# Moving the accumulating transfers of the value projection from ahead of unit 4 to between units 8 and 17

## The reference, cut to what matters

```python
h = rmsnorm(x, pre_norm_g[l])                       # 512 tokens x 2048
proj = jnp.einsum('btd,dn->btn', h, w_in[l])        # 2048 x 7168
q, fz, iv, gate_a, u, ug, gate_b = jnp.split(proj, split_pts, axis=-1)
o_a = hgrn2_mixer(q, fz, iv, lower_bounds[l], hg_norm_g[l]) * jax.nn.silu(gate_a)
o_b = conformer_conv(u, ug, dw_k, dw_b, ln_g, ln_b) * jax.nn.silu(gate_b)
y = jnp.einsum('btm,md->btd', jnp.concatenate([o_a, o_b], -1), w_out[l])
x = x + rmsnorm(y, post_norm_g[l])
```

## Time and profile before

| | |
|---|---|
| time before, median of 3 runs | 862.48 us (861.43 to 863.76) |
| the profiled execution's own time | 862.48 us |
| its span | 860.8 us |
| PE busy | 847.0 us, 98% of the span |
| DVE, ACT, POOL busy | 643.1, 446.8, 402.5 us |
| chain that ended last | PE 95% |
| transfers | 119.15 MB; q1 (issued by SP) 88.24 MB, q0 (issued by POOL) 25.17 MB |

### The profile page before, as it was taken

How to read it: one execution, slowest core, us unless ns; L and a number is a source line. 1 busy time by engine, 2 the same in 40 slices (tenths; PEclk the granted TensorE clock), 3 DMA queues, 4 the chain that set the end, 5 groups by cost and what they waited for, 6 DMA issues and landing times.

```text
span 860.8 us, 12144 instructions
## 1 busy us (share of the span) xinstructions
PE 847.0 (98%) x4162; PEld 711.1 (83%) x4162; DVE 643.1 (75%) x1033; ACT 446.8 (52%) x692; POOL 402.5 (47%) x209
## 2 busy tenths in 40 slices
PE   8989999999999999999999999999999999999996
PEld 7978888888888888888888888888888888888885
DVE  5559779998989994957759486684947893787557
ACT  7843434444433357646647565474646843555442
POOL 3579688799747345342533425244242445032000
PEclk9999999999999999999999999999999999999998
DMA  9999875879404323141331314223131247888945
GB/s 308 256 226 223 216 171 132 199 179 203 144 26 127 93 75 115 57 122 50 98 97 49 97 53 119 72 73 97 53 117 49 74 162 200 225 144 174 270 193 195
DMA packets 127135, 119.15 MB, mean 138 GB/s; under 512 B 3408, under 2 KB 102009, under 8 KB 124537
## 3 DMA queue, kind: packets, MB, share of 16 engines
q1 hardware_dynamic: 117289, 88.24, 33.8%
q0 software_dynamic: 9056, 25.17, 16.0%
q10 hardware_dynamic: 752, 5.25, 1.6%
HBM read 103.96 MB, written 4.19 MB: 126 GB/s over the span
## 4 chain that ended last, share of the span: by engine, by line
PE 95%; POOL 2%; ACT 1%; issue 1%; DMA 1%; DVE 1%; SPq 0%; DVEq 0%; ACTq 0%; POOLq 0%
PE banks L1700 20%; PE banks L1702 19%; PE banks L1701 19%; PE banks L1733 6%; PE banks L1732 6%; PE banks L1734 6%; PE banks L1843 3%; PE banks L1844 3%; PE banks L1845 3%; PE banks L1764 1%; PE banks L1754 1%; PE banks L1612 1%; PE banks L1770 1%; PE banks L1798 1%; POOL w_lo L524 1%
## 5 line engine op out<-in xcount | busy, mean ns | idle before, releaser
L524 POOL TENSOR_TENSOR w_lo<-w_raw,w_hi 128x1024 fp32r<-128x1024 f32 x122 | 308.4, 2533 | 318.6 <-ACT w_hi L660 298.6
L1700 PE MATMUL banks<-h_hi,w_hi 128*128 128x512 f32 x736 | 292.3, 397 | 2.2 <-POOL w_lo L524 2.2
L1702 PE MATMUL banks<-h_hi,w_lo 128*128 128x512 f32 x736 | 287.8, 391 | 0.0
L1701 PE MATMUL banks<-h_lo,w_hi 128*128 128x512 f32 x736 | 287.4, 391 | 0.0
L1162 DVE SCALAR_TENSOR_TENSOR banks<-work,tap,banks 128x512 f32<-128x512 f32 x238 | 179.8, 755 | 7.9
L1700 PEld LDWEIGHTS banks<-h_hi,w_hi 128*128 128x128 f32 x736 | 138.8, 189 | 30.5 <-DVE work L1206 2.4
L660 ACT ACTIVATE w_hi<-w_raw 128x1024 fp32r<-128x1024 f32 x104 | 109.4, 1052 | 105.1 <-PE banks L1702 57.1
L1702 PEld LDWEIGHTS banks<-h_hi,w_lo 128*128 128x128 f32 x736 | 138.5, 188 | 29.3
L1701 PEld LDWEIGHTS banks<-h_lo,w_hi 128*128 128x128 f32 x736 | 138.8, 189 | 28.1 <-issue 0.5
L1843 PE MATMUL banks<-w_hi,h_hi 128*128 128x512 f32 x128 | 50.9, 397 | 0.0
L1845 PE MATMUL banks<-w_hi,h_lo 128*128 128x512 f32 x128 | 49.9, 390 | 0.0
(11 more groups left out here) (232 smaller groups left out, 1303.5 us busy)
## 6 DMA issues: line engine op xcount, KB each, us to landing
w_raw<-in_w_in SPq DMA_DIRECT2D x112, 512.0 KB, 3.8
w_raw<-in_w_out SPq DMA_DIRECT2D x32, 512.0 KB, 5.2
gates<-in_w_in POOLq DMA_DIRECT2D x12, 512.0 KB, 7.6
work<-in_w_out POOLq DMA_DIRECT2D x12, 512.0 KB, 10.1
work<-h_hi POOLq DMA_DIRECT2D x4, 1024.0 KB, 9.6
work<-h_lo POOLq DMA_DIRECT2D x4, 1024.0 KB, 10.6
mix<-in_x ACTq DMA_DIRECT2D x4, 1024.0 KB, 10.5
out_y<-mix SPq DMA_DIRECT2D x3, 1024.0 KB, 3.9
```

The source lines that it names most:

```text
L524: g.tensor_tensor(w_lo[:, a], w_raw[:, r * UW:(r + 1) * UW], w_hi[:, a].bitcast(fp32), ALU.subtract).then_inc(lo_done, 1)
L1700: mm(o, wh, hh, start=kt == 0, stop=False)
L1701: mm(o, wh, hl, start=False, stop=False)
L1702: ins = mm(o, wl, hh, start=False, stop=kt == KT - 1)
```

## The change

The four `v_bsum` loads are spread: one each after SP's load of units 8, 9, 10, 11. The two minus token adds go from ahead of unit 4 to behind the `w_lo` of units 8 and 9, the four P5 weight adds behind units 10, 11, 14, 16. The other four early token adds move as well: late_high_hi from 8 to 12, late_high_lo from 13 to 15, early_low_hi from 16 to 13, early_low_lo from 20 to 17. ACT makes the three negated copies behind its `w_hi` of units 6, 7 and 8, in the order first, minus, then, and both minus adds wait for all three. Nothing is added or removed in what is computed.

```diff
-    S_ADDS_AFTER = {8: ("then", "late_high_hi", 32), 13: ("then", "late_high_lo", 48),
-                    16: ("first", "early_low_hi", 32), 20: ("first", "early_low_lo", 48),
+    S_ADDS_AFTER = {8: ("first", "minus", 16), 9: ("then", "minus", 16), 12: ("then", "late_high_hi", 32),
+                    13: ("first", "early_low_hi", 32), 15: ("then", "late_high_lo", 48), 17: ("first", "early_low_lo", 48),
...
+        ADDS_AFTER[(10, 11, 14, 16)[u]] = ("P5", u)
...
-    BSUM_AFTER = 6
+    BSUM_AFTER = {8 + u: u for u in range(KT // 4)}
...
-                    pool.wait_ge(v_turned, 3 if to == "then" else 2)
+                    pool.wait_ge(v_turned, 3)
...
-            for u in range(HU):
-                v_add_weights("P5", u)
-            v_add_tokens("first", "minus", 16)
-            v_add_tokens("then", "minus", 16)
...
-            act.wait_ge(x_lo, 2 * KT)
-            A(v_minus, late_low_lo, ACT.Copy, scale=-1.0).then_inc(v_turned, 1)
-            A(v_first, late_low_hi, ACT.Copy, scale=-1.0).then_inc(v_turned, 1)
-            act.wait_ge(par_t, 1)
-            A(v_then, late_low_hi, ACT.Copy, scale=-1.0).then_inc(v_turned, 1)
...
+                if s == 4:
+                    act.wait_ge(x_lo, 2 * KT)
+                    act.wait_ge(par_t, 1)
+                    A(v_first, late_low_hi, ACT.Copy, scale=-1.0).then_inc(v_turned, 1)
+                if s == 5:
+                    A(v_minus, late_low_lo, ACT.Copy, scale=-1.0).then_inc(v_turned, 1)
+                if s == 6:
+                    A(v_then, late_low_hi, ACT.Copy, scale=-1.0).then_inc(v_turned, 1)
```

More of the change, by code:

```diff
@@ L431, in conv_load @@
                         in_unit(n, r % RING, half, (COL_UG if name == "UG" else COL_U) + j * P)
-                if n == BSUM_AFTER:
+                if n in BSUM_AFTER:
+                    u = BSUM_AFTER[n]
                     sp.wait_ge(x_ss, 3)
-                    for u in range(HU):
-                        sp.dma_start(v_bsum[u].rearrange("p (k c) -> p k c", c=512),
-                                     w_in[0, v_rows(u), ds(COL_V2, 512)].rearrange("(k p) c -> p k c", p=P)).then_inc(v_in[u], 16)
+                    sp.dma_start(v_bsum[u].rearrange("p (k c) -> p k c", c=512),
+                                 w_in[0, v_rows(u), ds(COL_V2, 512)].rearrange("(k p) c -> p k c", p=P)).then_inc(v_in[u], 16)
             def x_load(tt):
@@ L732, in _ @@
                 x_hi_part(1, k)
-            late_low_hi, late_low_lo = (quarter(h, 1, 0).bitcast(fp32) for h in (h_hi, h_lo))
-            act.wait_ge(x_lo, 2 * KT)
-            A(v_minus, late_low_lo, ACT.Copy, scale=-1.0).then_inc(v_turned, 1)
-            A(v_first, late_low_hi, ACT.Copy, scale=-1.0).then_inc(v_turned, 1)
-            act.wait_ge(par_t, 1)
-            A(v_then, late_low_hi, ACT.Copy, scale=-1.0).then_inc(v_turned, 1)
             act.wait_ge(lb_v, 1)
@@ L769, in v_turn @@
             def v_turn(s):
+                late_low_hi, late_low_lo = (quarter(h, 1, 0).bitcast(fp32) for h in (h_hi, h_lo))
+                if s == 4:
[6 more added lines that the diff above has]
+                    A(v_then, late_low_hi, ACT.Copy, scale=-1.0).then_inc(v_turned, 1)
                 if s == 27:
```

## The result

The changed kernel takes 869.32 us (median of 5 runs, 867.4 to 872.36), the kernel before 862.48 us in the same sitting (5 runs, 861.43 to 863.76). The ratio is 1.0077, with a 95% interval from 1.0050 to 1.0103: slower by 0.8%. Forecast were 867.0 us, own range 864 to 869, wide range 858.0 to 868.5. The sign and the place of the loss are as forecast; the time lies above both ranges.

A forecast was written before the change was run, and what follows sets the result against it. PE was taken as the bound, in flight for 98% of the span. 862.5 - 2.3 (unit 4 wait) - 1.7 (clock) + 6.8 (unit 14 wait) + 1.7 (clock) = 867.0 us; range 864 to 869, wide 858.0 to 868.5.

The forecast's parts named there:

- The wait at unit 4: PE's wait for weights ahead of unit 4 goes, as ACT's copies no longer stand ahead: 2.3 us gained.
- The clock there: PE's slow clock behind its wait at unit 4 should not occur: 1.7 us gained.
- A: First minus token add, behind unit 8 in POOL's queue: issued at 57.3, landing at 65.7 us.
- B: Second minus token add, behind unit 9 in POOL's queue: issued at 62.1, landing at 70.9 us.
- w0: First P5 weight add, behind unit 10 in POOL's queue: issued at 66, landing at 73.5 us.
- w1: Second P5 weight add, behind unit 11 in POOL's queue: issued at 69.5, landing at 76.1 us.
- C: Token add late_high_hi, behind unit 12 in POOL's queue: issued at 73, landing at 81.4 us.
- D: Token add early_low_hi, behind unit 13 in POOL's queue: issued at about 78, landing at 86.6 us.
- Rival 1: Loads hold their share beside POOL's adds, PE never waits after unit 3: 858.5 us, chance 0.32.
- The wait: PE waits at unit 14 for its load, held by POOL's adds and landing at 88.0: 6.8 us lost.
- Rival 2: Short waits of 1 to 4 us at unit 14 or units 15 to 18: 862.5 us, chance 0.17.
- rival 3: The wait at unit 4 stays and the queue does no harm: 862 us, chance 0.05.

The follow-up runs named there:

- e2: Changed kernel with the four v_bsum loads and four P5 weight adds back where the kernel before has them: 859.12 us, ratio 0.9958.
- e5: Changed kernel with e2's edits, and early_low_hi and early_low_lo behind units 18 and 22 in place of 13 and 17: 858.7 us.
- e9: Kernel before with 10 idle matmuls on PE ahead of unit 4: 862.08 us, ratio 0.9994.
- e3: Changed kernel with each token add issued as two transfers with 2 KB rows in place of one with 8 KB rows: 874.59 us.
- e6: Changed kernel with early_low_hi issued behind unit 14 in place of unit 13: 872.13 us, ratio 1.0114.
- e10: Changed kernel run again unedited, against the kernel before: 871.67 us, ratio 1.0093.

## Why the prediction was wrong in its number

- **The wait at unit 4: right.** 2.4 us gained for 2.3, and in e2 and e5 the whole gain of units 4 and 5 arrives at the end.
- **The clock there: right.** 1.7 us gone by the earlier trace rows; e9 measured 1.6 for the same stretch.
- **The copies, the `v_bsum` loads, POOL's issues: right.** PE has no wait from 44 to 84 us.
- **The landings: A right (65.7), the rest too early.** B was put at 70.9, w0 73.5, w1 76.1, C 81.4, D 86.6, and they came at 73.0, 76.2, 81.6, 86.8 and 92.0. C and D follow at 5.2 us as counted; 2.1 us were lost before B and 2.8 before w1, and there POOL's queue pauses: 18 packets from 64 to 66 us (189 of SP's beside them) and 85 from 74 to 76 (714).
- **The step that failed: "POOL's queue has no gap from about 60 to 86", and with it "some 750 of unit 14's 1024 have gone when D ends".** One for one held wherever both queues were at work, included (76 to 76 from 52 to 55 us). But in the pause at 74 to 76 the load took most of its packets, and 962 of 1024 had gone by 76.7, ten us before D's forecast end. By that count there would have been no wait. The second thing that the count lacked made one: it runs over the whole queue, and the kernel waits for the sixteenth part, which fell behind and landed at 89.9. My 88.0 came close by two errors against each other, and that is luck.
- **Rival 1 rested on a misreading of the earlier trace rows.** The two us there are not an exchange: from 117 to 118 the load had 153 packets beside 16, and from 118 to 119 the add had 84 beside 24. Beside w1 SP's queue had 27.0% (77 to 80). Its own mark, 1024 packets before 80.6, was all but met at 76.7 (962), and PE waited all the same.
- **The wait: 8.8 us for 6.8, the term that puts the time off.** The load came 1.9 later than put down, PE was ready 0.5 earlier, and from landing to PE it took 3.5 and not 3.8 us. With the 0.3 us at unit 20 that is the 2.3 us between 867.0 and 869.3.
- **The clock behind it: right,** 1.8 for 1.7. The further wait of 0.3 us at unit 20 was not foreseen ("after D nothing more").
- **The range: too narrow at its top.** It had 8 us as the bound of the wait, and took no account of the spread that a load's last part brings. The changed kernel's own runs go from 865.1 to 872.4.

Rival 1's time, 858.5, is nearly what e5 and e2 show when no load is held (858.7 and 859.1), for another reason than it gave. Rival 2 (862.5) and rival 3 (862) are ruled out by the waits.

## What to carry to other kernels

Where a load on the path must come through beside large accumulating transfers of another queue, count the pauses of that queue, not its mean share: beside them the load here got one packet for each of theirs, and in two us of pause (74 to 76) 646 of its packets passed, against 290 in the 8.4 us from its issue until then. Leave a pause, or keep the other transfers off the stretch. Moving six transfers out of the way of one unit took away the empty stretch that another unit's load had. Count what each DMA engine has left when the next large transfer starts, since a load is worth its last part. A kernel whose times spread over 7 us where its neighbours' spread over 1 may hold such a race; its times alone already ask for a second profile.

## What the chip showed that was not expected

- A load with 0.5 KB rows gets one packet for each packet of POOL's accumulating transfers, whatever their rows: 81 to 81 beside 8 KB rows (0.05 MB to 0.61 MB, 80 to 83 us), 81 to 82 beside the 2 KB rows of a weight add (73 to 74), 244 to 263 beside token adds cut to 2 KB (e3, 85 to 88). In a pause it got 472 in one us (75 to 76). One load took 3.8 us alone and 24.3 here.
- Transfers that POOL has issued in time can still leave such a pause: w1, issued at 68.33, moved few packets before 76, with w0 through at 75.
- The sixteen parts of one load can land 14 us apart (75.7 and 89.9), and 1.2 to 10 us apart in executions that are the same up to there (e6, e10).
- POOL can stand 6.16 us in an issue (e3), with nothing in the program that it waits for. This and the two shorter stands there (until 67.33 and 80.18 us) ended 0.2 to 0.4 us after an earlier transfer of POOL's had landed (90.8, 67.1 and 79.8).
- Behind a stand of PE of 2.2 us the granted clock fell to its lower level for 3.4 us, and with work of no use in the same place (e9) it stayed at the upper one.
